# The first pair's token rows picked by TensorE with a 0/1 matrix instead of gathered by an indirect DMA

## The chip, the cores and the metric

The kernel runs on one core of one Trainium2 chip. The metric is the device time of one execution in microseconds (us).

## The reference

One inference step of a one-layer encoder in float32, for 512 prompt frames and 32 sample frames (544 tokens, model width 1024). A mixer (a state-space branch and a causal pooling branch, merged by gates) gives x2 = x + merged @ w_out. Then a mixture of experts follows, and only its routing matters here:

```python
xn = rmsnorm(x2, g)                       # g = g_ffn
lg = xn @ w_router_group                  # (n, 4); grp = argmax
le = einsum('nd,dge->nge', xn, w_router_expert)     # the group's 8 logits
top_v, top_i = top_k(le[n, grp], 2)
wk = softmax(top_v) * max(softmax(lg))
eidx = grp * 8 + top_i                    # two of 32 experts per token
for e in range(32):
    h = silu(xn @ w_gate[e]) * (xn @ w_up[e])       # 1024 -> 512
    y += combine[:, e] * (h @ w_down[e])            # 512 -> 1024
return x2 + y                             # then a final rmsnorm
```

## The kernel before, in words

The kernel is written by hand: each engine has its own program, and semaphores order them. Nothing plans the order; what an engine executes next is what stands next in its program, and a wait holds everything behind it on the same engine.

**Mixer.** The first 300 us compute the two branches, with 2 MB blocks of weights streamed into three slots.

**Output product and routing (304 to 395 us).** The tokens lie in five tiles, in the order 4, 0, 1, 2, 3 (`OUT_ORDER`, the 32 sample frames first). `out_part` (line 1558) multiplies one tile with w_out in eight parts on TensorE; DVE adds the residual in place (`residual`, 1176), so that `x_tok` then holds x2. Between the parts of a tile stand the routing steps of the tile before: `turn_x2` and `logits` (1567, 1578), `choose` on DVE (1200), `ranks` on TensorE (1588: a product with a triangular matrix gives each token its rank at its expert), `slots` on DVE (1233: the rank as a 0/1 row over 64 slots), `slot_ids` and `slot_values` on TensorE (1598, 1606: products that put token numbers, weights and norms into the experts' slots). DVE adds these up over the tiles (`take_ids`, `take_values`, 1259 and 1263). Expert e has 64 slots; two experts make a pair, 128 rows.

For the last tile there is no product left to fill TensorE, and `keep_busy` (1644) issues filler products of 128x512 whose result nothing reads: 4 before the last ranks, 3 after the last slot ids, 2 after the last slot values.

DVE then turns the slot ids into row numbers (1285 to 1292), signals `rows_ready`, takes the values of tile 3, makes and takes the values of the last tile and signals `slot_w_ready`.

**First pair.** POOL has stored each tile of x2 to DRAM (`x2_rows`, 542 to 544). Once all are stored and the row numbers are there, it gathers the pair's 128 rows with an indirect DMA (`gather`, 546) into `xg`. TensorE waits for it (1710), transposes the two halves (`turn_half`, 1662), and DVE multiplies with g while it takes them out of PSUM (1304 to 1308).

**Experts.** The loop at 1716 runs over 32 experts: `gate_up` (1680: both products of 64 tokens, 32 of 128x512 records), ACT copies the result with the norm as scale (`gate_up_out`, 757, after one wait for `slot_w_ready` at 766), `turn_gate_up`, silu and product (`hidden`, 1329), `down` of the expert before, DVE scales the result (`result`, 1334) and POOL scatters it. The next pair's rows are gathered meanwhile.

**Weights.** Each expert has three loads of 2 MB (gate, up, down) from SP, into a ring of eleven slots (`RING`, 92). The first ten are loaded as their places come free during the output product; the eleventh lies where `x_tok` is and waits for the first gather (403). From the twelfth on a load waits for the product that used its slot before: `gu_done` for gate and up, `down_done` for down. The twelfth and thirteenth wait for the first `gate_up`, the fourteenth for the first `down`.

Of the kernel before, what the change touches and what calls it, by code (L numbers as in the profile page):

```python
# [15 lines left out]
ALU = mybir.AluOpType  # L16
# [5 lines left out]
P = 128  # L22
# [97 lines left out]
def encoder_step(nc, a, out):  # L120
    ctx = ExitStack()
    with ctx:
# [8 lines left out]
        def sem(name):  # L131
            return ctx.enter_context(nc.semaphore(name))

        def at(offset, words, rows=P, row0=0):
            return arena[row0:row0 + rows, offset:offset + words]
# [71 lines left out]
        junk1 = at(O_GB, D)  # L207
        ring = [at(o, SLOT) for o in RING]
        xg = at(O_XG, D)
        xg_t = at(O_XGT, D).rearrange("p (k t) -> p k t", k=KD)  # L210
        gu_rows = [at(O_GU + n * F, F) for n in range(2)]
        h = [at(o, 4 * TILE).rearrange("p (k t) -> p k t", k=4) for o in O_H]
# [39 lines left out]
        unused, ids = small(NE), small(NE)  # L252
        y_row, x_row = small(NE).bitcast(I32), small(NP).bitcast(I32)
        slot_w = small(2, NE)
        counts = small(NE)
        ov_f, ov_entry = small(TT, 2), small(TT, 2, 4)
        ov_row = small(TT, 2).bitcast(I32)
# [34 lines left out]
        xg_in = [sem("xg_in0"), sem("xg_in1")]  # L292
        w_arr = [sem(f"expert_w_in{n}") for n in range(NS)]
        last_in = [sem(f"last_gate_up_in{n}") for n in range(4)] + [sem(f"last_down_in{n}") for n in range(2)]
        xt_done, xt_ready = sem("xg_turned"), sem("xg_t_ready")
        gu_done, gu_copied, gu_turned = sem("gate_up_done"), sem("gate_up_copied"), sem("gate_up_turned")
        silu_ready, h_ready, down_done, y_ready = sem("silu_ready"), sem("h_ready"), sem("down_done"), sem("y_ready")
# [39 lines left out]
        def _(sp):  # L337
# [62 lines left out]
            sp.wait_ge(out_done, 2 * TT)  # L400
            for l in range(EARLY + 1, NS - 1):
                load(l)
            sp.wait_ge(xg_in[0], 16)
            load(NS - 1)
            def freed(l):
                e, kind = divmod(l - NS, 3)
# [50 lines left out]
        def _(pool):  # L457
# [65 lines left out]
            for m in range(8):  # L523
# [6 lines left out]
            pool.wait_ge(emptied["dve"], emptied_by("dve", NUM["po7"]))  # L530
            pool.iota(slot_no, pattern=[[0, 2], [1, TILE]], base=0, channel_multiplier=0,
                      allow_small_or_imprecise_dtypes=True)
            pool.iota(prefer, pattern=[[-1, NE]], base=NE, channel_multiplier=0, allow_small_or_imprecise_dtypes=True)
            pool.iota(ebase, pattern=[[EXTRA * TILE, NE]], base=0, channel_multiplier=0,
                      allow_small_or_imprecise_dtypes=True)
# [15 lines left out]

            pool.wait_ge(x2_stored, 16 * TT)
            pool.wait_ge(rows_ready, 1)
            gather(0)
            pool.wait_ge(xt_done, 2)
            gather(1)
            for e in range(NE):
                j = e // 2 + 2
# [44 lines left out]
        def _(act):  # L603
# [109 lines left out]
            def square(n, half):  # L713
                i = OUT_ORDER[n]
                act.wait_ge(x2_ready, 2 * n + half + 1)
                if n or half:
                    act.wait_ge(squares2, 2 * n + half)
                act.activation(junk1[:ROWS[i], half * F:(half + 1) * F], x_tok[:ROWS[i], i, half * F:(half + 1) * F],  # L718
                               ACT.Square, accum_out=(ss, ss2)[half][:ROWS[i], i:i + 1]).then_inc(squares2, 1)

            def turned_out(n, half):
# [39 lines left out]
            def gate(par, turned):  # L761
                act.wait_ge(gu_turned, turned)
                src = ps[:, 4 + par, :].rearrange("p (k t) -> p k t", k=4)
                act.activation(h[par], src[:, :, 0:TILE], ACT.Silu).then_inc(silu_ready, 1)  # L764

            act.wait_ge(slot_w_ready, 1)
            for e in range(NE):
                if e >= 2:
# [30 lines left out]
        def _(dve):  # L799
# [8 lines left out]
            def tt(out_, x0, x1, op):  # L808
                step(dve.tensor_tensor(out_, x0, x1, op))  # L809
# [423 lines left out]
            def slots(n):  # L1233
                i = OUT_ORDER[n]
                r = ROWS[i]
                dve.wait_ge(chosen_ready, n + 1)
                dve.wait_ge(rank_done, n + 1)
                tt(rank_mul[:r], onehot[:r, i], ps[:r, 7, P:P + NE].unsqueeze(1).to_broadcast((r, 2, NE)), ALU.mult)
                step(dve.tensor_reduce(rank[:r, i], rank_mul[:r], X, ALU.add))
                for k in range(2):  # L1240
                    last = dve.tensor_scalar(slot_hot[n % 2][:r, k], slot_no[:r].rearrange("p h s -> p (h s)"),
                                             rank[:r, i, k:k + 1], None, ALU.is_equal)
                last.then_inc(hot_ready, 1)
                dve.tensor_tensor(before[:r], before[:r], chosen[n % 2][:r], ALU.add).then_inc(before_ready, 1)
                dve.wait_ge(before_ready, n + 1)
# [46 lines left out]
            last.then_inc(rows_ready, 1)  # L1292
            take_values(TT - 2)
            values(TT - 1)
            take_values(TT - 1)
            dve.sem_inc(slot_w_ready, 1)

            def x_out(turned, t=P):
                dve.wait_ge(xt_done, turned)
# [5 lines left out]
            for n in range(2):  # L1305
                dve.wait_ge(xt_done, n + 1)
                dve.tensor_tensor(xg_t[:, :, n * TILE:(n + 1) * TILE], ps[:, n, :].rearrange("p (k t) -> p k t", k=KD),
                                  g_x.unsqueeze(2).to_broadcast((P, KD, TILE)), ALU.mult).then_inc(xt_ready, 1)
            dve.wait_ge(count_done, 1)
            step(dve.tensor_copy(counts, ps[:, 7, 256:256 + NE]))  # L1310
            for j in range(EXTRA):
# [70 lines left out]
        def _(pe):  # L1382
# [241 lines left out]
            for n in range(1, TT):  # L1624
# [16 lines left out]
                    turn_x2(n, 0)  # L1641
                out_part(n, 7)
                slot_ids(n - 1)
            def keep_busy(times):

                for _ in range(times):
                    pe.matmul(ps[:, 3, :], ident, g_b[:, 0:F], start=True, stop=True)  # L1647

            logits(TT - 1, 0)
            turn_x2(TT - 1, 1)  # L1650
            logits(TT - 1, 1)
            pe.wait_ge(squares2, 2 * TT)
            keep_busy(4)
            ranks(TT - 1)
            slot_values(TT - 2)
            slot_ids(TT - 1)
            keep_busy(3)
            slot_values(TT - 1)
            keep_busy(2)


            def turn_half(n):

                blocks = xg.rearrange("t (q k) -> t k q", k=KD)
                part = slice(n * TILE, (n + 1) * TILE)
                for k in range(KD):
                    last = pe.transpose(ps[:, n, k * TILE:(k + 1) * TILE], blocks[part, k, :], ident[part, part])
                last.then_inc(xt_done, 1)
# [38 lines left out]
                    pe.wait_ge(arrived_at, count)  # L1707
                return view

            pe.wait_ge(xg_in[0], 16)  # L1710
            turn_half(0)
            turn_half(1)
            pe.wait_ge(rows_ready, 1)
# [2 lines left out]
            for e in range(NE + 1):  # L1716
                if e < NE:
                    pe.wait_ge(xt_ready, e + 1 if e < 2 else e // 2 + 2)
                    if e >= 2:
                        pe.wait_ge(gu_copied, e - 1)  # L1720
                    gate_up(e % 2, xg_t[:, :, e % 2 * TILE:(e % 2 + 1) * TILE], weights(e, 0), weights(e, 1), e + 1 == NE)
                    if e % 2 and e + 1 < NE:
                        j = e // 2 + 1
                        pe.wait_ge(xg_in[j % 2], 16 * (j // 2 + 1))
                        turn_x(P)
                if e:
                    pe.wait_ge(h_ready, e)
                    if e >= 3:
                        pe.wait_ge(y_ready, e - 2)
                    if e == 1:  # L1730
                        pe.wait_ge(slot_w_ready, 1)
                    if e == 2:
                        pe.wait_ge(counts_ready, 1)
                    down((e - 1) % 2, weights(e - 1, 2), e == NE)
                if e < NE:
                    pe.wait_ge(gu_copied, e + 1)
                    if e >= 2:
                        pe.wait_ge(h_ready, e - 1)
                    turn_gate_up(e % 2)
# [60 lines left out]
```

## Time and profile before

| | us |
|---|---|
| median of the timed runs | 899.69 |
| the runs | 899.69, 899.43, 899.92 |
| the profiled execution, its own time | 893.66 |
| its span, first to last instruction | 892.1 |
| TensorE busy (matmuls) | 798.9 (90%) |
| DVE, ACT, POOL busy | 262.9, 120.1, 128.1 |
| mean granted TensorE clock | 0.964 of full |

All durations of the prediction come from the one profiled execution. Its time is the span and a little around it; the timed runs are separate executions. A busy share is a mean over stages with different limits, so it doesn't say what bounds a stage: the stretches, the queue of SP and the waits do.

### The profile page before, as it was taken

How to read it: one execution, taken by the hardware profiler on the slowest of the kernel's cores; microseconds unless marked ns; L12 is line 12 of the kernel's file. 1: busy time of each engine (PE TensorE's matmuls, PEld its weight loads, DVE VectorE, ACT ScalarE, POOL GpSimd, SP SyncE). 2: the span in 40 equal slices, each digit the busy share in tenths (PEclk: the TensorE clock that was granted, in tenths of full speed). 3: DMA queues.
4: the chain of work that ended last, by engine and by line, in shares of the span. 5: the costliest groups of instructions: out<-in, count | busy, mean ns of one | idle time of the engine just before them, and what ended most of it. 6: DMA issues, size and time to landing. Idle time of an engine off the chain costs nothing.

```text
span 892.1 us, 9599 instructions
## 1 busy us (share of the span) xinstructions
PE 798.9 (90%) x3864; PEld 451.9 (51%) x3865; DVE 262.9 (29%) x741; ACT 120.1 (13%) x230; POOL 128.1 (14%) x224
## 2 busy tenths in 40 slices
PE   3999999999999899989999779779777977878986
PEld 2888888778888655543333333333223333333332
DVE  4899668320011245551111011111101111110115
ACT  5010021120000133320000000000000000000012
POOL 3000007850023300010111010000101000010000
PEclk9999999999999999999999998889899999998999
DMA  8522022344200393388999999999999999999946
GB/s 303 149 95 95 1 106 49 100 161 156 95 1 0 126 428 160 121 311 306 432 424 429 427 426 427 428 427 425 428 426 425 426 427 428 423 428 427 407 175 251
DMA packets 42671, 251.58 MB, mean 282 GB/s; under 512 B 13173, under 2 KB 14025, under 8 KB 29922
## 3 DMA queue, kind: packets, MB, share of 16 engines
q1 hardware_dynamic: 35436, 237.49, 65.3%
q0 software_dynamic: 6672, 12.86, 4.0%
q8 instruction: 31, 0.51, 0.2%
q10 hardware_dynamic: 518, 0.60, 0.2%
q14 instruction: 14, 0.11, 0.0%
HBM read 245.33 MB, written 13.46 MB: 290 GB/s over the span
## 4 chain that ended last, share of the span: by engine, by line
PE 64%; DMA 32%; DVE 1%; issue 1%; ACT 1%; ACTq 1%; SPq 0%; POOLq 0%; DVEq 0%
DMA arena<-in_w_exp_up 30%; PE ps L1416 26%; PE ps L1685 13%; PE ps L1562 6%; PE ps L1700 6%; PE ps L1761 2%; PE ps L1501 1%; PE ps L1496 1%; PE ps L1584 1%; PE ps L1675 1%; PE ps L1550 1%; PE ps L1692 1%; DMA arena<-y_parts 1%; PE ps L1647 1%; ACTq L605 1%
## 5 line engine op out<-in xcount | busy, mean ns | idle before, releaser
L1685 PE MATMUL ps<-arena 128*64 128x512 f32 x1024 | 248.6, 641 | 62.2 <-DMA arena<-in_w_exp_up 62.2
L1416 PE MATMUL ps<-arena 128*128 128x272 f32 x1024 | 237.3, 393 | 0.0
L1416 PEld LDWEIGHTS ps<-arena 128*128 128x128 f32 x1024 | 194.0, 190 | 39.7
L1685 PEld LDWEIGHTS ps<-arena 128*64 128x64 f32 x1024 | 84.4, 148 | 203.7 <-issue 202.3
L1700 PE MATMUL ps<-arena 128*64 128x512 f32 x512 | 116.4, 595 | 1.0 <-DVE arena L1332 1.0
L1336 DVE TENSOR_SCALAR arena<-ps,arena 128x512 f32<-128x512 f32 x32 | 24.0, 750 | 214.8 <-PE ps L1700 214.8
L809 DVE TENSOR_TENSOR arena<-arena 128x256 f32<-128x256 f32 (+10 forms) x213 | 73.9, 347 | 11.0 <-ACT arena L718 3.9
L1700 PEld LDWEIGHTS ps<-arena 128*64 128x64 f32 x512 | 37.9, 137 | 64.4 <-issue 61.4
L1301 DVE TENSOR_TENSOR arena<-ps,arena 128x1024 f32<-128x1024 f32 x15 | 18.4, 1224 | 173.4 <-PE ps L1675 173.4
L563 POOL DMA_INDIRECT y_parts<-arena x32 | 31.9, 998 | 250.3 <-DVE arena L1336 250.3
L759 ACT ACTIVATE arena<-ps,arena 128x512 f32<-128x512 f32 x32 | 22.0, 687 | 307.8 <-PE ps L1685 307.8
L1562 PE MATMUL ps<-arena 128*128 128x512 f32 x128 | 59.6, 603 | 0.0
L547 POOL DMA_INDIRECT arena<-x_rows,arena x16 | 16.6, 1039 | 183.7 <-PE ps L1675 166.9
L1562 PEld LDWEIGHTS ps<-arena 128*128 128x128 f32 x128 | 22.8, 190 | 21.7 <-issue 21.5
L1160 DVE TENSOR_TENSOR arena<-ps,arena 128x544 f32<-128x544 f32 x8 | 5.8, 723 | 88.7 <-PE ps L1416 88.7
L1692 PEld LDWEIGHTS ps<-arena 128*128 128x128 f32 x128 | 17.8, 208 | 26.9 <-issue 25.2
L661 ACT ACTIVATE arena<-ps 128x544 f32<-128x544 f32 x20 | 12.5, 624 | 133.1 <-PE ps L1416 133.1
L764 ACT ACTIVATE arena<-ps 128x256 f32<-128x256 f32 x32 | 12.3, 383 | 125.5 <-PE ps L1692 125.5
L1761 PE MATMUL ps<-arena 128*128 128x512 f32 x48 | 22.8, 635 | 2.6 <-issue 2.3
L1692 PE MATMUL ps<-arena 128*128 128x128 f32 x128 | 23.9, 309 | 0.8 <-ACT arena L759 0.8
L525 POOL TENSOR_TENSOR arena<-arena 128x544 f32<-128x544 f32 x8 | 10.7, 1336 | 90.1 <-DVE arena L1160 90.1
L1675 PEld LDWEIGHTS ps<-arena 128*128 128x128 f32 x120 | 14.5, 194 | 12.2 <-issue 12.2
(228 smaller groups left out, 492.3 us busy)
## 6 DMA issues: line engine op xcount, KB each, us to landing
arena<-in_w_exp_gate SPq DMA_DIRECT2D x31, 2048.0 KB, 42.7
arena<-in_w_exp_up SPq DMA_DIRECT2D x31, 2048.0 KB, 32.6
arena<-in_w_exp_down SPq DMA_DIRECT2D x31, 2048.0 KB, 37.8
arena<-in_w_in SPq DMA_DIRECT2D x6, 2048.0 KB, 9.2
arena<-in_x_prompt SPq DMA_DIRECT2D x8, 512.0 KB, 6.4
arena<-in_w_out SPq DMA_DIRECT2D x2, 2048.0 KB, 10.4
arena<-y_parts SPq DMA_DIRECT2D x4, 1024.0 KB, 8.3
arena<-in_w_glu_a SPq DMA_DIRECT2D x1, 2048.0 KB, 10.5
```

The source lines that it names most:

```text
L563: pool.indirect_dma_start(out=y_parts, out_offset=bass.IndirectOffsetOnAxis(ap=y_row[:, e:e + 1], axis=0), in_=y_sb[e % 2], in_offset=None ...
L759: act.activation(gu_rows[par], ps[:, 2 + par, :], ACT.Copy, scale=scale).then_inc(gu_copied, 1)
L809: step(dve.tensor_tensor(out_, x0, x1, op))
L1301: dve.tensor_tensor(xg_t[:, :, 0:t], src[:, :, 0:t], g_x.unsqueeze(2).to_broadcast((P, KD, t)), ALU.mult).then_inc(xt_ready, 1)
L1336: dve.tensor_scalar(y_sb[par], ps[:, 6 + par, :], scale, None, ALU.mult).then_inc(y_ready, 1)
L1416: last = pe.matmul(dst[:, hh, 0:HALF], w[:, k, m * P:(m + 1) * P], rhs[:, k, hh * HALF:(hh + 1) * HALF], start=(k == 0), stop=(k == kk - 1))
L1562: last = pe.matmul(ps[:, 2 * (n % 2) + half, :], m_t[:, k, i * P:(i + 1) * P], (w0, w1)[half][:, k, :], start=(k == 0), stop=(k == 7))
L1675: last = pe.transpose(*turned)
L1685: last = pe.matmul(ps[n * TILE:(n + 1) * TILE, 2 + par, :], x_t[:, k, :], w[:, k, :], start=(k == 0), stop=(k == KD - 1))
L1692: last = pe.transpose(ps[:, 4 + par, k * P:(k + 1) * P], blocks[:, k, :], ident)
L1700: last = pe.matmul(ps[half * TILE:(half + 1) * TILE, 6 + par, :], h[par][:, k, :], w_down[:, k, half * F:(half + 1) * F], start=(k == 0), ...
L1761: last = pe.matmul(ps[:, 2 * i + half, :], ident, part[:, half * F:(half + 1) * F], start=first, stop=end)
```

## The change

Each tile's DVE step gets two more 0/1 matrices, `first_hot[n]`: for experts 0 and 1, a row per token and a column per slot (64 each, 128 together). `first_at` is (rank + 1) where the token has chosen the expert and 0 elsewhere; it is compared with 1 to 64. TensorE multiplies this matrix with the tile's x2 rows, still in SBUF, and sums over the five tiles in two PSUM banks: the result is the 128 rows of the first pair. Two tiles are picked ahead of the last ranks, three behind them, ahead of the last slot ids. The fillers are gone. ACT copies the two banks to SBUF, and the transposes read that. The first gather is gone; POOL's first is the one of pair 1, after the picks (its place overlaps the last tile of `x_tok`), and the counts on its semaphores follow. SP's eleventh load waits for the picks and the stores instead of the gather. The last `slot_values` moves behind the first `gate_up` on TensorE, and its taking behind the scaling of the first pair on DVE. POOL makes one more row of constants. ACT's squares both write to the first half of their scratch.

```diff
+        xg_first = x2_t[1].rearrange("p k t -> p (k t)")
...
+        first_at, slot_1 = small(2), small(TILE)
+        first_hot = [small(P)] + [at(O_GB + F + n * P, P) for n in range(4)]
...
@@ SP
-            sp.wait_ge(xg_in[0], 16)
+            sp.wait_ge(x2_stored, 16 * TT)
+            sp.wait_ge(picked, 2)
             load(NS - 1)
@@ POOL
+            pool.iota(slot_1, pattern=[[1, TILE]], base=1, channel_multiplier=0, allow_small_or_imprecise_dtypes=True)
...
             pool.wait_ge(x2_stored, 16 * TT)
             pool.wait_ge(rows_ready, 1)
-            gather(0)
-            pool.wait_ge(xt_done, 2)
+            pool.wait_ge(picked, 2)
             gather(1)
@@ ACT
+            for half in range(2):
+                act.wait_ge(picked, half + 1)
+                act.activation(xg_first[:, half * F:(half + 1) * F], ps[:, 2 + half, :], ACT.Copy).then_inc(first_rows, 1)
             act.wait_ge(slot_w_ready, 1)
@@ DVE, in slots(n)
                 dve.wait_ge(rank_done, n + 1)
+                stt(first_at[:r], ps[:r, 7, P:P + 2], 1.0, chosen[n % 2][:r, 0:2], ALU.add, ALU.mult)
+                for e in range(2):
+                    last = dve.tensor_scalar(first_hot[n][:r, e * TILE:(e + 1) * TILE], slot_1[:r], first_at[:r, e:e + 1],
+                                             None, ALU.is_equal)
+                last.then_inc(pick_ready, 1)
                 tt(rank_mul[:r], onehot[:r, i], ps[:r, 7, P:P + NE].unsqueeze(1).to_broadcast((r, 2, NE)), ALU.mult)
...
             take_values(TT - 2)
             values(TT - 1)
-            take_values(TT - 1)
-            dve.sem_inc(slot_w_ready, 1)
...
                 dve.tensor_tensor(xg_t[:, :, n * TILE:(n + 1) * TILE], ps[:, n, :].rearrange("p (k t) -> p k t", k=KD),
                                   g_x.unsqueeze(2).to_broadcast((P, KD, TILE)), ALU.mult).then_inc(xt_ready, 1)
+            take_values(TT - 1)
+            dve.sem_inc(slot_w_ready, 1)
             dve.wait_ge(count_done, 1)
@@ TensorE
-            def keep_busy(times):
-
-                for _ in range(times):
-                    pe.matmul(ps[:, 3, :], ident, g_b[:, 0:F], start=True, stop=True)
+            def pick(n, halves=(0, 1)):
+
+                i = OUT_ORDER[n]
+                r = ROWS[i]
+                pe.wait_ge(pick_ready, n + 1)
+                pe.wait_ge(x2_ready, max(2 * n + 2, 2 * TT - 2))
+                for half in halves:
+                    last = pe.matmul(ps[:, 2 + half, :], first_hot[n][:r], x_tok[:r, i, half * F:(half + 1) * F],
+                                     start=(n == 0), stop=(n == TT - 1))
+                    if n == TT - 1:
+                        last.then_inc(picked, 1)
 
             logits(TT - 1, 0)
             turn_x2(TT - 1, 1)
             logits(TT - 1, 1)
-            pe.wait_ge(squares2, 2 * TT)
-            keep_busy(4)
+            pick(0)
+            pick(1)
             ranks(TT - 1)
+            for n in range(2, TT):
+                pick(n)
             slot_values(TT - 2)
             slot_ids(TT - 1)
-            keep_busy(3)
-            slot_values(TT - 1)
-            keep_busy(2)
...
-                blocks = xg.rearrange("t (q k) -> t k q", k=KD)
+                blocks = xg_first.rearrange("t (q k) -> t k q", k=KD)
...
-            pe.wait_ge(xg_in[0], 16)
+            pe.wait_ge(first_rows, 2)
             turn_half(0)
             turn_half(1)
...
                     gate_up(e % 2, xg_t[:, :, e % 2 * TILE:(e % 2 + 1) * TILE], weights(e, 0), weights(e, 1), e + 1 == NE)
+                    if e == 0:
+                        slot_values(TT - 1)
```

## Rows read from the trace of the kernel before

**Rows 1.** The page, bytes moved in 40 equal slices of the span.
```profile
GB/s 303 149 95 95 1 106 49 100 161 156 95 1 0 126 428 160 121 311 306 432 424 429 427 426 427 428 427 425 428 426 425 426 427 428 423 428 427 407 175 251
```

**Rows 2.** Stretches; columns: us, busy time and instructions per engine, clock, DMA share, GB/s.
```profile
404.00:405.00 1.00, 0.15 (x2) 0.00 (x1) 0.00 (x0) 0.69 (x1) 0.00 (x0) 1.00 0.00 0
...
416.00:417.00 1.00, 1.00 (x8) 0.27 (x4) 0.00 (x0) 0.00 (x0) 0.00 (x0) 1.00 0.61 139
...
420.00:450.00 30.00, 30.00 (x144) 10.86 (x142) 3.57 (x5) 2.83 (x5) 3.15 (x4) 1.00 1.01 427
```

**Rows 3.** Timeline of SP, the issues of weight loads; columns: start us, duration us, instruction.
```profile
395.09 0.33 SPq L390 DMA_DIRECT2D arena<-in_w_exp_up  x1
404.19 0.33 SPq L390 DMA_DIRECT2D arena<-in_w_exp_down  x1
...
417.48 0.33 SPq L390 DMA_DIRECT2D arena<-in_w_exp_up  x1
```

**Rows 4.** Timeline from the last slot ids to the first product of the experts.
```profile
388.33 0.63 PE L1602 MATMUL ps<-arena 128*128 128x32 f32 x4 [0.69 <-DVE arena L1241]
...
391.16 1.09 POOL L547 DMA_INDIRECT arena<-x_rows,arena  x1 [11.50 <-DVE arena L1291]
...
391.58 0.23 DVE L1256 TENSOR_SCALAR arena<-arena 128x32 f32<-128x32 f32 x1
...
395.12 1.59 PE L1667 MATMUL ps<-arena 64*128 64x64 f32 x16 [0.82 <-DMA arena<-x_rows,arena]
396.32 1.29 DVE L1307 TENSOR_TENSOR arena<-ps,arena 128x512 f32<-128x512 f32 x2 [3.54 <-PE ps L1667]
...
397.06 7.09 PE L1685 MATMUL ps<-arena 128*64 128x512 f32 x32
```

**Rows 5.** Timeline, rows that give prices: products, copies and DVE's operations.
```profile
365.19 0.22 DVE L1266 TENSOR_TENSOR arena<-arena,ps 128x64 f32<-128x64 f32 x1 [1.90 <-PE ps L1612]
...
368.39 5.40 PE L1562 MATMUL ps<-arena 128*128 128x512 f32 x12
...
376.42 0.60 ACT L727 ACTIVATE arena<-ps 128x512 f32<-128x512 f32 x1 [0.67 <-PE ps L1574]
...
381.49 5.32 PE L1647 MATMUL ps<-arena 128*128 128x512 f32 x8
...
387.01 0.64 PE L1612 MATMUL ps<-arena 128*128 128x64 f32 x4
...
387.79 0.48 DVE L1241 TENSOR_SCALAR arena<-arena 128x128 f32<-128x128 f32 x2
```

**Rows 6.** The chain that ended last: one small group among the products (start, us).
```profile
364.69 0.39 PE ps L1612 x4
```

**Rows 7.** Timeline: DVE's wait for a product of tile 2, and after the first product.
```profile
359.97 0.69 DVE L1182 TENSOR_TENSOR arena<-ps,arena 128x512 f32<-128x512 f32 x1 [1.05 <-PE ps L1562]
...
402.82 0.17 DVE L1327 COPY arena<-arena 128x10 f32<-128x10 f32 x1
...
404.26 0.69 ACT L759 ACTIVATE arena<-ps,arena 128x512 f32<-128x512 f32 x1 [16.30 <-PE ps L1685]
...
406.20 0.42 DVE L1332 TENSOR_TENSOR arena<-ps,arena 128x256 f32<-128x256 f32 x1 [3.21 <-ACT arena L764]
```

**Rows 8.** TensorE's clock: stretches, then later first products with the idle before them.
```profile
378.10:381.49 3.39, 2.70 (x26) 2.46 (x24) 1.70 (x8) 2.33 (x5) 0.53 (x1) 0.98 0.75 203
381.40:384.80 3.40, 3.40 (x6) 1.58 (x6) 2.88 (x15) 0.46 (x1) 0.00 (x0) 0.50 0.98 417
394.30:397.06 2.76, 1.93 (x18) 1.75 (x18) 0.74 (x2) 0.00 (x0) 0.00 (x0) 1.00 0.43 88
...
536.38 9.76 PE L1685 MATMUL ps<-arena 128*64 128x512 f32 x32 [5.05 <-DMA arena<-in_w_exp_up]
...
755.01 7.09 PE L1685 MATMUL ps<-arena 128*64 128x512 f32 x32 [3.22 <-DMA arena<-in_w_exp_up]
...
770.53 8.75 PE L1685 MATMUL ps<-arena 128*64 128x512 f32 x32 [3.08 <-DMA arena<-in_w_exp_up]
```

**Rows 9.** The gathers' line (POOL), the last line of its answer.
```profile
DMA to landing us min/median/max: 3.9/10.7/12.0
```

More of the change, by code:

```diff
@@ L294, in encoder_step @@
         last_in = [sem(f"last_gate_up_in{n}") for n in range(4)] + [sem(f"last_down_in{n}") for n in range(2)]
+        pick_ready, picked, first_rows = sem("first_hot_ready"), sem("first_rows_picked"), sem("first_rows_ready")
         xt_done, xt_ready = sem("xg_turned"), sem("xg_t_ready")
@@ L717, in square @@
                     act.wait_ge(squares2, 2 * n + half)
-                act.activation(junk1[:ROWS[i], half * F:(half + 1) * F], x_tok[:ROWS[i], i, half * F:(half + 1) * F],
+                act.activation(junk1[:ROWS[i], 0:F], x_tok[:ROWS[i], i, half * F:(half + 1) * F],
                                ACT.Square, accum_out=(ss, ss2)[half][:ROWS[i], i:i + 1]).then_inc(squares2, 1)
@@ L1721, in _ @@
                     gate_up(e % 2, xg_t[:, :, e % 2 * TILE:(e % 2 + 1) * TILE], weights(e, 0), weights(e, 1), e + 1 == NE)
+                    if e == 0:
+                        slot_values(TT - 1)
                     if e % 2 and e + 1 < NE:
                         j = e // 2 + 1
-                        pe.wait_ge(xg_in[j % 2], 16 * (j // 2 + 1))
+                        pe.wait_ge(xg_in[j % 2], 16 * ((j + 1) // 2))
                         turn_x(P)
```

## The prediction

> **What bounds the kernel now.** I read the 40 slices first: from slice 20 on the transfers stay at about 427 GB/s to the end of the expert loop [rows 1], which streams the experts' weights. The table of stretches says where that begins: nothing moves at 404 to 405 us, 139 GB/s at 416 to 417, 427 from 420 us on [rows 2]. A kernel whose last 400 us run at one constant rate ends earlier only if that stream begins earlier or carries less, so I looked for what starts it.
>
> SP's timeline [rows 3] gives the order: the eleventh load (up weights of expert 3) at 395.09, the next two from 404.19, the next three from 417.48. The queue has run low when the load of 417.48 comes, and these three are 6.3 MB, 14.7 us at 427 GB/s; after them it is never dry. The load at 417.48 waits for the end of the first `down`. So the rule I price with: **the end moves by as much as the end of the first `down` moves.** TensorE's own order ties that to the first `gate_up`: 397.06 to 417.48, 20.4 us [rows 3, 4].
>
> The path to 397.06 now [rows 4]: last slot ids on TensorE 388.33 to 388.96; DVE makes the token numbers of them; POOL issues the gather at 391.16; it has landed for the transposes at 395.12; DVE scales from 396.32; `gate_up` 397.06. DVE meanwhile makes the last values (done 391.81), hidden behind the gather.
>
> **The change, part by part.**
>
> *Removed: the first gather.* From its issue to the first transpose 3.96 us [rows 4]. On this the Trainium skill, "DMA: Bandwidth & Descriptors" (section "Anatomy of one DMA — SWDGE (gpsimd) path"), fits 2.0 us + bytes/436e3; for this gather of 0.5 MB that is, as an estimate of mine, 3.2 us. By the page the wait removed would be worth some 0.8 us less than by the row. The row decides, and the sum below starts from the measured 397.06 and needs neither. The 0.5 MB less to move gain nothing: they moved while the queue had room.
>
> *Removed: nine filler products; added: ten picking products*, all of 128x512. Four fillers stood before the last ranks, and picks 0 and 1 are four products too, so I leave the ranks where they are. The first group behind them starts at 387.01 [rows 5]. There now come three picks, six products, twelve records; twelve such records take 5.40 us from first start to visible result [rows 5]. So the second half shows at 392.4, the first two records (0.9 us) earlier. Pick 0 has 32 rows only; no row has this shape, so it lies between nothing and the full price, and I take the full one. Then come the values of tile 3 and the last slot ids; a group of this kind adds 0.39 us [rows 6]: 392.4 + 0.8 = **393.2 for the last slot ids, where it was 388.96**. This is the step I watch most: the ids are now queued behind the picks.
>
> *Added on ACT:* two copies of 128x512 out of PSUM, 0.60 us each [rows 5]; the second ends at 392.45 + 0.6 = 393.05. The transposes follow at 393.1, two us before the old 395.12, and the first half is visible to DVE 1.2 us later (395.12 to 396.32) at 394.3.
>
> *DVE's queue.* `take_ids`, the row numbers, the values of tile 3 and those of the last tile all stand ahead of the scaling. From the end of the ids that run took 388.96 to 391.81, 2.85 us [rows 4]. It now ends at **396.05**, well behind the 394.3 of the transposes. Scaling to `gate_up` is 0.74 us: `gate_up` starts at **396.8, 0.3 us earlier**. So the gather's wait is replaced almost whole by DVE's work, which used to lie under it.
>
> *Moved: last slot values behind the first product.* ACT's first copy needs `slot_w`. Before, it started 7.20 us after `gate_up` [rows 4, 7]. Now: `gate_up` 7.09, the group of small matmuls 0.39, hand-over to DVE 0.11 (365.08 to 365.19), DVE's add 0.22 [rows 5, 6], its own wait and the signal 0.1, an estimate: 7.9 us. **+0.7 us** before the turned products, `gate_up` 1 and the first `down`.
>
> *DVE behind it.* The chain that counts and prepares the overflow (397.61 to 402.99 [rows 4, 7], 5.4 us) begins some 7.9 us after `gate_up`, at 404.7, and lasts to 410.1; the first `hidden` moves from 406.20 to about 410.2. The first `down` reads it after `gate_up` 1 and the transposes of pair 1, 0.4 us later than the 413.8 of before: some 3.5 us of cover, 0 on the path; were the cover gone, `down` would slip by the excess.
>
> *Added on DVE per tile:* one small fused operation and two comparisons of 128x64, between 0.23 for one of 128x32 and 0.48 for the pair of 128x128 [rows 4, 5]: 0.6 to 0.7 us in all, five times. For tiles 0 to 3 DVE's next wait on TensorE is at least 1.05 us long [rows 7] and hides it. In the last tile it delays the hot rows to about 389, needed at 392.8. 0. One more iota on POOL stands before the routing constants; DVE waits for the first product of the stage after them: 0.
>
> *Queues.* SP's eleventh load waits for the picks, not the gather: 392.5 for 395.09. It lands by 399.5, and the queue stands idle until the next two loads either way, as at 404 to 405 us now; 0, with -2.6 as the bound if the stream could follow it. POOL issues the gather of pair 1 some 2.1 us after the ids, at 395.4 for 397.52, read at 412.7; hidden even at the 10.7 us median of the gathers [rows 9]. Loads 12 and 13 come 0.3 us earlier into an empty queue: 0.
>
> *TensorE's clock.* Between the last pick (392.4) and `gate_up` (396.8) there are now 4.4 us with small matmuls, transposes and 1.5 us of idle. Rows on both sides [rows 8]: 394.30 to 397.06, 2.8 us of that sort, and the granted clock stayed at 1.00; after 378.10 to 381.49, 3.4 us, it stood at 0.50 (1.2 of 2.4 GHz) from 381.4 to 384.8, and eight filler records took 5.32 us [rows 5] for the 3.68 that eight take by the twelve (5.40 less four of 0.43): 1.64 us. In the expert loop `gate_up` took 7.09 us after an idle of 3.22, 8.75 after 3.08 and 9.76 after 5.05 [rows 8]. So the cost lies between 0 and 2.7 us. The nearest row is the 1.64 of a slow stretch of 3.4 us spent wholly on dense work; one that begins while the transposes still run is half over when `gate_up` starts. I take half, **+0.8**.
>
> Sum: -0.3 + 0.7 + 0.8 = **+1.2 us** on the end of the first `down`, and so on the end. The profiled execution took 893.66 us (span 892.1), so 894.9 for one like it. The three timed runs have a median of 899.69, 6.0 us above it; no row tells where these 6 us lie, and I carry the difference over: **900.9 us**, +0.13%. What a measurement of this kernel can tell from no change is about 0.2%, 1.8 us.
>
> **The rivals.**
>
> *Slower: the clock falls for the whole first product.* Place: the first `gate_up`. Price 1.64 to 2.67 us instead of 0.8, so +2.0 to +3.1: 901.7 to 902.8. For it: the new gap is longer than the 3.4 us that did it before. Against: the 2.8 us gap at the same place did no harm, and an idle of 3.22 didn't either. It decides from a clock cost of 1.4 us.
>
> *Faster: the gather is dearer in the timed runs.* It landed in 3.9 us in the profile, the least of the sixteen, whose median is 10.7 [rows 9], and the timed runs are 6.0 us longer. With 10.7, the old `gate_up` would start 6.8 us later and the change bring 5.6 us net: 894.1. It decides from a gather of 6.9 us. Against: the other gathers run beside the full weight stream, this one while the queue was nearly empty.
>
> *No change: DVE doesn't hold the scaling.* Should `gate_up` start as soon as the transposes allow (394.3 + 0.74 = 395.0), the sum is 1.8 us less: 899.1. The program order speaks against it.
>
> *The change doesn't do what it says:* the eleventh load or the first rows wait as before for another thing (the store of x2). The first gather had the same wait and was issued at 391.16, before 392.4, so this costs nothing: 900.9 again.
>
> **How the numbers follow.** The forecast with the third and fourth case 0.58; the slower rival 0.28; the dearer gather, with anything else that removes more than 1.8 us, 0.14. The range: below, no clock cost (+0.4) and half of DVE's 1.8 us gone besides, with -0.5 for a gather a little dearer, -1.0; above, the whole 2.67, +3.1: 898.7 to 902.8. The far side of the gather rival is what is left out.
>
> **What would show it.** Right: last slot ids near 393.2; DVE busy from there to 396 without a gap, its scaling right behind; `gate_up` within 0.5 us of 396.8; ACT's first copy 7.9 us behind it; the load after the first `down` at 417.9 or later, from there 427 GB/s as before; the granted clock below 1.00 somewhere in 393 to 400. Wrong: `gate_up` before 395.5, or DVE waiting for transposes right before the scaling; or an end that moves by something else than that load does.

## The result, and the profile after

The changed kernel has a median of 900.10 us in 20 timed runs, the kernel before 898.63 us in 20 beside them. The ratio is 1.0033, with a 95% interval of 1.0016 to 1.0049: some 3 us slower. In a second comparison (x1_repeat, below) it was 1.0050 (1.0032 to 1.0067). The single executions spread far more than the three of before that stood ahead of the prediction: 893 to 914 us for the kernel before, 898 to 905 for the changed one.

The profiled execution has a span of 898.8 us, 6.7 more than before. The page of the changed kernel, the slices that answer to [rows 1]:

```profile
GB/s 310 139 94 70 25 106 41 107 134 181 94 1 0 107 427 174 117 319 218 425 427 425 426 426 427 428 425 427 428 426 427 426 427 427 425 428 426 408 190 246
```

The second half is as before, one constant rate. SP's timeline of the changed kernel, issues of the weight loads, as in [rows 3] (start us, duration us):

```profile
307.26 0.35 SPq L394 DMA_DIRECT2D arena<-in_w_exp_gate  x1
...
375.16 0.33 SPq L394 DMA_DIRECT2D arena<-in_w_exp_up  x1
382.92 0.33 SPq L394 DMA_DIRECT2D arena<-in_w_exp_down  x1
...
396.50 0.33 SPq L394 DMA_DIRECT2D arena<-in_w_exp_up  x1
410.56 0.33 SPq L394 DMA_DIRECT2D arena<-in_w_exp_down  x1
...
424.67 0.33 SPq L394 DMA_DIRECT2D arena<-in_w_exp_up  x1
```

These issues cut the span into stages. The same of the kernel before:

```profile
304.03 0.35 SPq L390 DMA_DIRECT2D arena<-in_w_exp_gate  x1
...
370.38 0.33 SPq L390 DMA_DIRECT2D arena<-in_w_exp_up  x1
378.14 0.33 SPq L390 DMA_DIRECT2D arena<-in_w_exp_down  x1
```

| stage | before, us | after, us | difference |
|---|---|---|---|
| start to first expert load (mixer) | 304.03 | 307.26 | +3.2 |
| to the ninth load (end of the output product) | 74.11 | 75.66 | +1.6 |
| to the load behind the first `down` | 39.34 | 41.75 | **+2.4** |
| from there to the end | 474.6 | 474.1 | -0.5 |

The change touches the third stage; in the second it adds small work on DVE and POOL alone, and x1_repeat below has the 74.1 us of before there. The first stage varies in both kernels (304.0 to 306.3 in the three profiles of kernels built on before, 304.0 to 307.4 in the eleven built on the change). I call the third stage **the stage** from here on. Its path in the changed kernel, from the timeline; it answers to [rows 4] and [rows 7]:

```profile
386.31 3.89 PE L1664 MATMUL ps<-arena 32*128 32x512 f32 x8
...
390.55 0.41 PE L1606 MATMUL ps<-arena 128*128 128x32 f32 x2 [0.34 <-DVE arena L1233]
...
391.01 5.40 PE L1664 MATMUL ps<-arena 128*128 128x512 f32 x12
...
396.64 0.58 PE L1615 MATMUL ps<-arena 128*128 128x32 f32 x4
...
397.15 1.59 PE L1686 MATMUL ps<-arena 64*128 64x64 f32 x16
...
397.33 0.19 DVE L817 TENSOR_TENSOR arena<-arena,ps 128x32 f32<-128x32 f32 x1 [4.42 <-PE ps L1615]
...
399.83 0.23 DVE L1269 TENSOR_SCALAR arena<-arena 128x32 f32<-128x32 f32 x1
...
399.98 1.28 DVE L1318 TENSOR_TENSOR arena<-ps,arena 128x512 f32<-128x512 f32 x2
...
400.71 9.80 PE L1704 MATMUL ps<-arena 128*64 128x512 f32 x32 [1.63 <-DVE arena L1318]
...
410.44 0.66 PE L1625 MATMUL ps<-arena 128*128 128x64 f32 x4
...
411.14 0.22 DVE L1279 TENSOR_TENSOR arena<-arena,ps 128x64 f32<-128x64 f32 x1 [9.88 <-PE ps L1625]
411.45 0.69 ACT L764 ACTIVATE arena<-ps,arena 128x512 f32<-128x512 f32 x1 [14.41 <-DVEq L1321]
```

To be seen: the last slot ids (L1615) stand right behind the twelve records of the picks; DVE, idle for 4.42 us till then, works without a gap from 397.33 to the scaling (L1318), while the transposes (L1686) have long been done; TensorE waits 1.63 us for it. Then the first `gate_up` takes 9.8 us (400.71 to 410.5) for 7.09 before. The stretches that say why (the clock is the third column from the end):

```profile
399.60:406.10 6.50, 5.38 (x14) 1.69 (x16) 1.66 (x6) 0.00 (x0) 0.91 (x1) 0.50 0.67 281
406.10:410.50 4.40, 4.40 (x22) 1.21 (x19) 0.00 (x0) 0.00 (x0) 0.00 (x0) 0.99 0.00 0
```

The granted clock was 0.50, 1.2 of 2.4 GHz, from 399.6 to 406.1; the whole slow stretch runs from 399.4 to 406.2, and 5.5 us of it lie over the product.

### The profile page after: what moved, and what is told of

The parts are those of the page before. It is cut to its first block, busy times and chain, and to the rows that moved or that the text cites. A ratio compares the mean times of both kernels' runs of the same rounds, so it can differ in the third digit from the quotient of the medians.

```text
span 898.8 us, 9625 instructions
## 1 busy us (share of the span) xinstructions
PE 808.4 (90%) x3866; PEld 454.2 (51%) x3867; DVE 265.3 (30%) x756; ACT 121.3 (13%) x232; POOL 127.2 (14%) x224
## 4 chain that ended last, share of the span: by engine, by line
PE 65%; DMA 30%; DVE 2%; issue 1%; ACT 1%; ACTq 1%; DVEq 0%
DMA arena<-in_w_exp_up 30%; PE ps L1429 26%; PE ps L1704 14%; PE ps L1575 6%; PE ps L1719 6%; PE ps L1782 3%; PE ps L1514 1%; PE ps L1509 1%; PE ps L1694 1%; PE ps L1563 1%; PE ps L1597 1%; PE ps L1711 1%; PE ps L1664 1%; PE ps L1634 1%; ACTq L610 1%
## 5 line engine op out<-in xcount | busy, mean ns | idle before, releaser
L1704 PE MATMUL ps<-arena 128*64 128x512 f32 x1024 | 254.4, 654 | 61.2 <-DMA arena<-in_w_exp_up 59.6
L1429 PE MATMUL ps<-arena 128*128 128x272 f32 x1024 | 239.7, 396 | 0.0
L1719 PE MATMUL ps<-arena 128*64 128x512 f32 x512 | 116.4, 595 | 1.0 <-DVE arena L1345 1.0
```

What stands on the lines that cost most here:

```text
L1429: last = pe.matmul(dst[:, hh, 0:HALF], w[:, k, m * P:(m + 1) * P], rhs[:, k, hh * HALF:(hh + 1) * HALF], start=(k == 0), stop=(k == kk - 1))
L1704: last = pe.matmul(ps[n * TILE:(n + 1) * TILE, 2 + par, :], x_t[:, k, :], w[:, k, :], start=(k == 0), stop=(k == KD - 1))
L1719: last = pe.matmul(ps[half * TILE:(half + 1) * TILE, 6 + par, :], h[par][:, k, :], w_down[:, k, half * F:(half + 1) * F], start=(k == 0), ...
```

## The experiments

The twelve runs, and the two profiles above, are read in the same way: times from the end of the output product (the issue of the ninth load), in one profiled execution each. "Load" is the one behind the first `down`; "slow" is how long the granted clock stayed down once it had fallen ahead of the ranks (in x3, x4 and v1 it came back only behind them).

| run | ranks | slow, us | first `gate_up` | its length | load | span after the load |
|---|---|---|---|---|---|---|
| before | 8.50 | 3.4 | 18.92 | 7.13 | 39.34 | 474.6 |
| before again | 8.51 | 3.4 | 18.93 | 7.12 | 39.34 | 474.7 |
| after | 7.63 | no fall | 17.79 | 9.85 | 41.75 | 474.1 |
| x1_repeat | 10.41 | 7 | 20.53 | 8.82 | 43.47 | 474.3 |
| x2_fill | 7.61 | no fall | 17.88 | 7.13 | 39.12 | 474.7 |
| x3_values_ahead | 10.91 | 10 | 22.15 | 7.13 | 42.56 | 474.9 |
| x4_ids_between | 9.90 | 7 | 19.74 | 7.13 | 40.99 | 474.5 |
| p1_short_last | 8.50 | 3.4 | 18.94 | 9.31 | 42.36 | 475.4 |
| p2_fillers_ahead | 8.51 | 3.4 | 22.31 | 7.13 | 43.56 | 474.9 |
| c1_all_three | 8.51 | 3.4 | 19.08 | 9.53 | 41.89 | 474.9 |
| u1_order_fill | 8.51 | 3.4 | 20.71 | 7.13 | 41.96 | 474.8 |
| c3_best | 7.61 | no fall | 17.11 | 7.13 | 37.52 | 474.9 |
| v1_short_fillers | 10.54 | 13 | 22.15 | 7.13 | 42.56 | 475.1 |
| c3_again | 7.63 | no fall | 17.12 | 7.13 | 37.53 | 475.8 |

(The length runs to the issue of the loads that wait for it. Of the experiments x1, c1, u1, v1 and c3 twice have timed runs as well; the others are one execution each.) The last column is within 1.7 us in fourteen executions whose stage differs by 6: the end does move with that load.

**x1_repeat** and **b1_before_again**: the two kernels unchanged.

> The changed kernel once more, to see what of its stage repeats. Measured from SP's issue of the ninth and tenth load (output product done) to the first gate_up, and from there to the load behind the first down. Theory (late ids, then DVE's queue, then a clock that falls in the gap): 17.8 us (18.7 if the picks themselves ran at half clock), gate_up 9.8 us long, 24.0 us to the load. Rival (the slow first gate_up was the chance of one execution): 17.8 us again, gate_up 7.1, 21.2 us to the load.

> The kernel before once more, for how its stage repeats. Theory: 38.5 us (clock full) to 39.5 (slow for 3.4 us under the fillers) from the end of the output product to the load behind the first down, and 474.5 us from there to the end of the span. Rival (its own stage varies as much as the changed kernel's): 41 us or more in this execution, and the difference of the timed runs lies elsewhere.

The kernel before repeats its stage to 0.01 us. The changed kernel doesn't: 43.47 for 41.75, since now the clock fell ahead of the picks as well. Timeline and stretches of the repeat:

```profile
381.50 7.23 PE L1664 MATMUL ps<-arena 32*128 32x512 f32 x8
388.51 0.36 PE L1606 MATMUL ps<-arena 128*128 128x32 f32 x2
...
388.94 5.40 PE L1664 MATMUL ps<-arena 128*128 128x512 f32 x12
```

```profile
381.40:388.60 7.20, 7.20 (x12) 2.60 (x11) 4.09 (x22) 2.48 (x6) 0.00 (x0) 0.53 0.98 416
388.60:398.60 10.00, 8.40 (x43) 5.31 (x41) 4.58 (x23) 1.19 (x2) 1.09 (x1) 1.00 0.56 213
398.60:402.10 3.50, 3.47 (x10) 1.13 (x12) 0.57 (x1) 0.00 (x0) 0.00 (x0) 0.54 0.90 380
```

The kernel before falls at the same place, after the small products of the logits, but only for 3.4 us [rows 8], and its eight filler records take 5.32 us [rows 5]. The picks' eight records took 7.23, and the ranks came 1.9 us later than before. The rival of the expectation, a slow first `gate_up` as the chance of one execution, would have had 7.1 us here; it was slow both times (9.85 and 8.82). How far chance has a part in it, x3 and p2 below tell.

**x2_fill**: dense work in the gap ahead of `gate_up`.

```diff
             pe.matmul(ps[:, 7, 256:256 + NE], ones, before, start=True, stop=True).then_inc(count_done, 1)
+            pe.wait_ge(w_arr[0], 16)
+            for _ in range(2):
+                pe.matmul(ps[:, 3, :], ident, ring[0][:, 0:F], start=True, stop=True)
```

> Two filler products of 128x512 between the transposes of the first pair and the first gate_up, where TensorE idles 1.6 us. Theory (the gap without dense work lets the clock fall): granted clock 1.00 during gate_up, gate_up 7.1 us, load behind the first down 2.4 us earlier relative to the end of the output product (39.3 for 41.75 us), gate_up's start later by at most 0.3. Rival (the fall has nothing to do with this gap): gate_up about 9.8 us as before, and 0.1 to 0.3 us added.

39.12, `gate_up` 7.13. No fall in this execution at all. Stretches of its stage:

```profile
383.00:400.90 17.90, 16.88 (x79) 9.86 (x77) 10.40 (x52) 5.95 (x12) 1.63 (x2) 1.00 0.86 326
400.90:408.00 7.10, 7.10 (x34) 2.27 (x33) 0.47 (x1) 0.00 (x0) 0.00 (x0) 1.00 0.45 188
```

The numbers are the theory's. That the two fillers kept the clock up isn't shown by it: without any filler in this gap the clock stayed at 1.00 in x3 and p2 as well, and in u1 it fell in spite of them.

**x3_values_ahead**: the last slot values ahead of `gate_up`.

```diff
+            slot_values(TT - 1)
             for e in range(NE + 1):
...
-                    if e == 0:
-                        slot_values(TT - 1)
```

> The last slot values back ahead of the first gate_up on TensorE, in the 1.6 us while DVE scales; DVE takes them behind the scaling as in the change. Theory (moving them behind the product cost 0.8 us): ACT's first copy follows the end of gate_up by 0.1 to 0.2 us instead of 0.95, start of gate_up the same within 0.2. Rival (DVE is behind anyway): the copy still comes 0.5 us or more after gate_up's end.

ACT's first copy started 7.20 us after `gate_up`, 0.07 behind its end, for 0.89 behind it in the changed kernel. The move costs 0.8 us, and TensorE had the room for it while DVE scales. In this execution the clock was down for 10 us from ahead of the picks on. It was back at 1.00 for the gap ahead of `gate_up` and stayed there, though no filler stood in that gap.

**x4_ids_between**: the ids are no longer behind all picks.

```diff
-            for n in range(2, TT):
-                pick(n)
+            pick(2)
             slot_values(TT - 2)
             slot_ids(TT - 1)
+            for n in range(3, TT):
+                pick(n)
```

> The values of tile 3 and the last slot ids between pick 2 and pick 3 instead of behind pick 4, so that DVE's row numbers and last values run under picks 3 and 4. Theory (the ids' place behind the picks holds the scaling up through DVE's queue): DVE done with its values before the transposes, gate_up 16.8 us after the end of the output product instead of 17.8 (1.0 us earlier), idle of TensorE ahead of gate_up under 1 us. Rival (the ACT copies and transposes set it): gate_up within 0.3 us of 17.8.

The absolute number is spoiled by the slow picks. Counted from the ranks, which come after them: `gate_up` 9.84 us behind for 10.16 in the changed kernel, although the picks' first products were still partly slow. The expectation was 1.0 us, so 0.3 came of it; some 0.5 us of the missing part is the slow clock behind the ranks (ranks to third pick 0.72 us for 0.46, third pick 2.17 for 1.96). Its timeline:

```profile
394.53 3.68 PE L1664 MATMUL ps<-arena 128*128 128x512 f32 x8
398.90 1.59 PE L1687 MATMUL ps<-arena 64*128 64x64 f32 x16 [0.69 <-ACT arena L773]
400.42 0.41 PE L1735 MATMUL ps<-arena 128*128 128x32 f32 x2
400.84 5.80 PE L1705 MATMUL ps<-arena 128*64 128x512 f32 x26
```

The transposes now wait for ACT, and `gate_up` follows them without a wait for DVE, 1.94 us behind their start as before [rows 4] instead of 3.56 us. So DVE's queue behind the late ids was the hold, as predicted; the second in line is ACT's copy.

**p1_short_last**: the order of the picks.

```diff
-            pick(0)
-            pick(1)
+            pick(1)
+            pick(2)
             ranks(TT - 1)
-            for n in range(2, TT):
+            for n in (3, TT - 1, 0):
                 pick(n)
```

> The order of the picks changed: tiles 0 and 1 (128 rows) ahead of the last ranks, then tiles 2, 3 and the sample tile (32 rows) behind them. In the repeat the granted clock fell just ahead of the picks and came back only after some 7 us, where the fillers of before were slow for 3.4 us. Theory A (the product with the 32-row matrix is why the clock comes back late): where the clock falls there, it is back after 3.4 us and the ranks start 8.5 us after the end of the output product. Theory B (the picks as such, 0/1 matrices that are mostly zero, or chance): it stays down 7 us or more and the ranks start at 10.4. If it doesn't fall there at all, the run tells neither.

The clock fell ahead of the picks and was back after 3.4 us, ranks at 8.50. Its eight records in slow and full clock:

```profile
385.19 4.98 PE L1664 MATMUL ps<-arena 128*128 128x512 f32 x8
390.01 0.30 PE L1606 MATMUL ps<-arena 128*128 128x32 f32 x2
```

This is what theory A asked for. `gate_up` was slow again (9.31); the gap ahead of it is untouched.

**p2_fillers_ahead**: the fillers back, all five picks behind the ranks.

```diff
-            pick(0)
-            pick(1)
+            pe.wait_ge(squares2, 2 * TT)
+            for _ in range(4):
+                pe.matmul(ps[:, 3, :], ident, g_b[:, 0:F], start=True, stop=True)
             ranks(TT - 1)
-            for n in range(2, TT):
+            for n in range(TT):
                 pick(n)
```

> The four filler products of before stand again ahead of the last ranks, and all five picks behind them. Theory (a fall of the clock ahead of the ranks is cut short by dense products, not by picks): slow stretch of 3.4 us as in the kernel before, ranks 8.5 us after the end of the output product, and two more picks on the path (3.4 us), so gate_up at 21.6 us. Rival (the length of the slow stretch has nothing to do with what runs in it): 7 us or more also here, ranks at 10.4.

3.4 us and ranks at 8.51, as the theory; 22.31 at `gate_up`, 0.7 us later than expected, for the two picks more on the path. Here the 32-row pick stood behind the ranks at full clock and did no harm.

The gap ahead of `gate_up` holds the same instructions as in the changed kernel, and yet the clock stayed at 1.00:

```profile
389.24 9.04 PE L1664 MATMUL ps<-arena 32*128 32x512 f32 x20
...
399.03 1.59 PE L1687 MATMUL ps<-arena 64*128 64x64 f32 x16
...
402.58 7.09 PE L1705 MATMUL ps<-arena 128*64 128x512 f32 x32 [1.62 <-DVE arena L1318]
```

From the end of the last product of 512 columns to the next one (`gate_up`, or the fillers in x2 and u1) there are 4.3 to 4.5 us in five executions: the clock fell in after, x1 and p1, not in x3 and p2. In c1 the gap was 3.7 us, and the clock fell. In the eight executions with 1.9 to 2.9 us (before twice, x2, x4, u1, v1, c3 twice) it fell once, in u1. So the longer gap goes with the fall, in four of six against one of eight, but doesn't decide it.

**v1_short_fillers**: the kernel *before*, its four fillers cut to 32 rows. No pick and no 0/1 matrix of the tokens is in it.

```diff
-            keep_busy(4)
+            for _ in range(4):
+                pe.matmul(ps[:, 3, :], ident[0:DEC], g_b[0:DEC, 0:F], start=True, stop=True)
```

> The kernel before with its four fillers ahead of the last ranks cut to 32 rows (the 32 upper rows of the same two operands); nothing else. Theory A (a product of 32 rows doesn't bring the clock back, whatever its values): where the clock falls ahead of them, it is down for 7 us or more instead of 3.4, ranks at 10.4 or later instead of 8.5, load behind the first down at 41 us or more for 39.3. Theory B (the mostly zero 0/1 matrix did it, or the picks' place): 3.4 us, ranks at 8.5, 39.3 as before.

Timeline and stretches:

```profile
383.86 7.19 PE L1654 MATMUL ps<-arena 32*128 32x512 f32 x8
390.98 0.64 PE L1593 MATMUL ps<-arena 128*128 128x32 f32 x2
...
394.07 4.47 PE L1647 MATMUL ps<-arena 128*128 128x512 f32 x6
```

```profile
386.50:390.00 3.50, 3.50 (x6) 1.33 (x4) 1.72 (x11) 1.81 (x4) 0.00 (x0) 0.50 0.97 410
390.00:393.50 3.50, 3.25 (x12) 2.08 (x10) 1.03 (x5) 0.25 (x2) 0.00 (x0) 0.50 0.98 411
```

Ranks at 10.54, load at 42.56: 3.2 us lost in the stage by the shape of four products whose result nothing reads. The clock came back only in the next run of 128-row fillers. The numbers are theory A's, in one execution, and nothing but the rows was changed. The timed runs don't show the loss, though: ratio 0.9996 (0.9974 to 1.0018, 10 runs against 23). How often each fall comes in the timed executions a few profiles can't say; this stays open.

**u1_order_fill**: the change with the order of p1 and the fillers of x2.

> The change with two edits aimed at the clock alone: the 32-row pick last (tiles 0 and 1 ahead of the ranks), and two filler products between the first pair's transposes and the first gate_up. Theory (the loss is TensorE's clock: a long slow stretch with the 32-row pick ahead of the ranks, and a fall in the gap before gate_up): ranks at 7.6 or 8.5 us after the end of the output product, gate_up 7.1 us long, load behind the first down at 39.1 to 40.0 (the kernel before: 39.3 twice; the changed kernel: 41.8 and 43.5); timed 0 to 0.1% above the kernel before. Rival (the static part, DVE's queue and the late slot values, is what costs): as the changed kernel, 0.3 to 0.5% above.

Load at 41.96, timed 1.0020 (1.0004 to 1.0036). The long stretch ahead of the ranks was gone. The gap ahead of `gate_up` was not cured: the clock fell as the transposes ended, and the two fillers took it instead of `gate_up` and pushed its start.

```profile
397.30 3.42 PE L1737 MATMUL ps<-arena 128*128 128x512 f32 x4
400.64 7.09 PE L1704 MATMUL ps<-arena 128*64 128x512 f32 x32
```

In x2 the same four records took 1.96 us. So the theory's numbers were missed: behind the ranks `gate_up` came at 12.20 for 10.27 in x2, 1.9 us lost. Of these 1.5 are the slow fillers themselves, a loss that they moved but didn't remove; 0.3 lie ahead of the transposes at full clock, where the picks with the 32-row one last took 5.59 us for 5.40 and the small group behind them 0.1 more.

**c1_all_three**: the order of p1, x3's values, and the ids behind the third pick.

> Three edits of the change together: picks of tiles 0 and 1 ahead of the ranks and the 32-row one last, values of tile 3 and last ids behind the third pick, last slot values ahead of the first gate_up. Theory: picks end 14.3 us after the end of the output product, gate_up at 17.0 (18.9 in the kernel before), ACT's copy 7.2 behind it, load behind the first down at 37.4 for 39.3 before; timed 1.5 to 2.5 us faster than the kernel before. Rival (the clock's falls eat it again): the load at 39 or later and a time no better than before.

The rival: 41.89, ratio 1.0009 (0.9987 to 1.0030). The transposes started at 16.04, 0.9 us earlier than before, but the clock fell as they ended; `gate_up` took 9.53, and the last slot values, now in front of it, 1.09 us instead of 0.6. With the ids early, nothing on DVE covers them there.

**c3_best**, and once more as **c3_again**: dense work in both holes, and little more on the path.

```diff
             logits(TT - 1, 0)
             turn_x2(TT - 1, 1)
+            pick(1, (0,))
             logits(TT - 1, 1)
-            pick(0)
-            pick(1)
+            pick(1, (1,))
+            pick(2)
+            pick(3, (0,))
             ranks(TT - 1)
-            for n in range(2, TT):
-                pick(n)
+            pick(3, (1,))
+            pick(TT - 1, (0,))
             slot_values(TT - 2)
             slot_ids(TT - 1)
+            pick(TT - 1, (1,))
+            pick(0)
+            pe.wait_ge(w_arr[0], 16)
+            pe.matmul(ps[:, 5, :], ident, ring[0][:, 0:F], start=True, stop=True)
...
             turn_half(0)
             turn_half(1)
+            slot_values(TT - 1)
```

(The slot values behind the first `gate_up` go; the start and stop flags of the picks follow the order. What the expectation calls half of pick 0 is `pick(1, (0,))` in the edit: pick 0 is the 32-row one.)

> A version meant to beat both: half of pick 0 (the tile of 128 rows) in TensorE's 0.7 us of idle between the last logits, three more halves ahead of the ranks, values of tile 3 and last ids behind two more halves, the rest and the 32-row pick, one filler while ACT copies, last slot values behind the transposes. Theory: ranks at 7.9 (clock kept) to 8.8, transposes at 14.5 to 15.4, gate_up at 16.5 to 17.4 and 7.1 us long, load behind the first down at 36.9 to 37.8 for 39.3; timed 0.15 to 0.3% faster than the kernel before. Rival (the clock falls somewhere again): 39 us or more, and no gain.

> The best version once more. Theory: 37.5 us from the end of the output product to the load behind the first down (37.0 to 38.4 if the clock falls ahead of the picks), 0.2 to 0.5% faster than the kernel before in the timed runs. Rival (the first result was the draw of the executions): within 0.1% of it.

Load at 37.52 and 37.53, the granted clock 1.00 throughout the stage both times. Timed 0.9948 (0.9929 to 0.9966) and 0.9968 (0.9951 to 0.9985) of the kernel before. Timeline of the first:

```profile
384.53 1.02 PE L1664 MATMUL ps<-arena 128*128 128x512 f32 x2
385.39 1.07 PE L1597 MATMUL ps<-arena 128*128 128x36 f32 x8
...
396.74 1.12 PE L1684 MATMUL ps<-arena 128*128 128x512 f32 x2
397.80 1.59 PE L1692 MATMUL ps<-arena 64*128 64x64 f32 x16
...
399.00 1.29 DVE L1318 TENSOR_TENSOR arena<-ps,arena 128x512 f32<-128x512 f32 x2 [2.24 <-PE ps L1692]
...
400.11 7.09 PE L1710 MATMUL ps<-arena 128*64 128x512 f32 x32
```

Half a pick (L1664, 384.53) lies where TensorE had idled 0.69 us between the last logits, and the logits behind it run on time; the filler (L1684) lies under ACT's copies. The version is faster than the kernel before, against which it was timed, and so by these ratios than the changed one too. Of its gain the stage explains 1.8 us of the 2.9 to 4.7; the rest isn't located. Whether the half pick and the filler kept the clock up, or the shorter path did, two executions can't say; of the twelve without a dense product between the logits, two kept it as well.

## Why the prediction was right or wrong

**The bound, right.** The time after the load behind the first `down` is 474.1 to 475.8 us in all profiles. What the stage gains or loses goes to the end.

**The static steps, right.** Counted from the ranks' start, so without the clock ahead of them, `gate_up` came at 10.16 (after) and 10.12 (repeat) for 10.42: 0.3 us earlier, as said. Twelve records took 5.40 us, DVE's run from the ids to the scaling 2.7 us without a gap, and the transposes began 2.8 us ahead of the scaling, of which 1.2 are their own [rows 4]; their result waited for DVE. The late slot values cost 0.82 us for the 0.7 of the sum. With the full clock everywhere (x2_fill) the stage took 39.12. The kernel before, had it been spared its 0.9 us of slow fillers, would have taken 38.45: the static part is some 0.7 us (0.1 of it the fillers of x2), where the sum had 0.4. The counting chain on DVE reached `hidden` at 416.75, well ahead of the `down` at 420.98, so its cover held.

**The clock, mis-sized: the step that failed.** The sum had +0.8 us, half of one slow stretch, with 0 to 2.7 as bounds. In the changed kernel's profile the first `gate_up` took 2.7 us more, the upper bound; in the repeat 1.7. The sum for the first is -1.13 (of this 0.87 because the clock happened not to fall ahead of the ranks) + 2.72 + 0.82 = +2.41 us, the measured difference of the stage. For the repeat it is 1.91 - 0.30 + 1.69 + 0.83 = +4.13. So what came is the slower rival, given 0.28: the forecast was +0.13%, within what can't be told from no change, the measured +0.33% and +0.50% are slower. The reasoning for a half took one stretch of 3.4 us that begins over the transposes. In the changed kernel's two profiles the clock fell after the transposes had ended. In the first it stayed down 6.8 us, twice the stretch of [rows 8], and 5.5 of them lay over `gate_up`; in the repeat 3.4 us, all of them over `gate_up`. At half the clock each costs half its length, 2.7 and 1.7. Why it falls in this gap in some executions and not in others (x3, p2) stays open.

That the median of 900.10 lies so near the forecast 900.9 is luck: that number was carried over from a median of three, 899.69, and the kernel before has 898.63 in twenty.

**The ranks, wrong in one execution of two.** "Picks 0 and 1 are four products too, so I leave the ranks where they are" took products as equal by their count and width. At full clock they nearly are: eight records, four of them of the 32-row pick, took 3.89 us, 3.68 with 128 rows only. On this the Trainium skill, "TensorE: Matmul & The Clock Gate" (section "Why this matters for your kernels"), says that a single matmul with 32 rows takes the same time as one with 128; the trace agrees, but for these 0.2 us. What the picks don't do is the fillers' other work. Where the clock had fallen ahead of them, it stayed down 7 to 13 us where 32-row products came first (x1, x3, x4, v1) and 3.4 us with 128-row products alone (before, before again, p1, p2, c1, u1). The sum had nothing for this: it was +1.91 us in the repeat, and -0.87 in the first profile, where the clock didn't fall.

**The faster rival** (a dearer gather in the timed runs) didn't come: the kernel before has its gather at the same 3.9 us in both profiles, and no timed comparison favours the change.

**Open.** The output product took 1.5 us or more longer in six of the eleven executions of kernels built on the change and in none of three built on the kernel before. Its first product was slow then (5.21 us at a mean clock of 0.69, for 3.66 at 1.00, in the first profile). TensorE's idle right ahead of that product is the same in both kernels, 2.87 us, so the extra constants on POOL don't lengthen it; nothing else was tried, and it may be the draw of the executions. Open too is how the timed 3.0 and 4.5 us split over the stages. Both profiles of the kernel before (893.66 and 894.11 us) are 4.5 us or more shorter than the medians around them, so none shows a usual execution of it, and stage and timed runs don't always go together: v1 lost 3.2 us in its stage and c1 2.6, but their ratios can't be told from 1.

## What to carry to other kernels

Let work that replaces a filler be as dense as the filler, in rows too, if it stands where the clock may have fallen, and put the short product where the clock is up (the profiles show the gain of this, the timed runs of v1 don't). Before a wait is removed, list what ran under it on the other engines; here DVE's 2.7 us came out from under the gather and took its place. And where one transfer stream bounds the rest, find the issue that starts it: the difference of two kernels can be read there to 0.1 us, when whole executions spread by several.

## What the runs showed of the hardware

- After the same stretch of small products (378 to 381 us in the kernel before) the granted clock fell to 0.50 in ten of fourteen executions. Four kept 1.00: both of c3, which have a product of 128 rows and 512 columns within it, and two of the twelve without one (after, x2).
- Where four products of 128 rows stood there, the clock was back 3.4 us after its fall, in six of six executions. With four of 32 rows, a slice of the identity, it was down for 13 us and came back only under the next products of 128 rows (v1, one execution). With two of 32 rows, a tokens' 0/1 matrix, and two of 128 behind them it was down for 7, 10 and 7 us (x1, x3, x4).
- In a gap of 4.3 to 4.5 us with transposes, small products and at most 1.6 us of idle the clock fell in three of five executions; once fallen it was down for 3.4 us (x1) or 6.8 us (after, p1), most of it under `gate_up`'s products of 128 rows and 64 tokens.
- At the full clock 32 rows cost no less than 128: 3.89 us for eight records, four of them of 32 rows, for 3.68.
